# The expert layers of a two-block transformer kernel, as two phases with a scratch in DRAM between them

## The chip, the cores and the metric

The kernel runs on one NeuronCore of a Trainium2 chip (one of eight; the others are idle). The metric is the device time of one execution in microseconds (us). Engines are named as the profile names them: PE (TensorE) multiplies matrices, PEld is its weight load, DVE is VectorE, ACT is ScalarE, POOL is GpSimd, SP is SyncE, which here only issues DMAs. A kernel's launch is one program with one instruction stream for each engine; the streams are ordered by semaphores alone, written out by hand.

## The reference, cut to what matters

Two blocks follow one another. The first has two layers (DEPTH = 2), and each of them ends in a product-key mixture of experts over T = 256 tokens of width D = 1024. A query finds, for each token and each of 8 heads, 16 of 128 x 128 experts and their softmax weights:

```python
def one_block(xblk):
    q = (xblk @ w_query).reshape(B, TOKEN_BLOCK, N_PEER_HEADS, 2, SUBKEY_DIM)
    s = jnp.einsum('bthpd,hpnd->bthpn', q, sub_keys).astype(jnp.float32)
    vals, idx = lax.top_k(s, PEER_TOPK)
    ...
    top_s, pos = lax.top_k(cand, PEER_TOPK)
    eidx = jnp.take_along_axis(cand_idx, pos, axis=-1)
    g = jax.nn.softmax(top_s, axis=-1).astype(xblk.dtype)
    h = jnp.einsum('btd,bthkd->bthk', xblk, expert_u[eidx])
    act = jax.nn.gelu(h, approximate=False) * g
    return jnp.einsum('bthk,bthkd->btd', act, expert_v[eidx])
```

The kernel gathers nothing. It multiplies all tokens with all 16384 rows of `expert_u` (128 tiles of 128 experts), takes the gelu, multiplies with a dense gate (tokens x experts, zero where an expert wasn't chosen) and multiplies the result with all rows of `expert_v`. Beside that there are modulation vectors: `silu(c) @ ada_w` for both blocks, matrices of 1024 x 6144 and 1024 x 9216 per layer.

## The kernel before, in words

**Weights.** Every weight comes as units of 128 partitions x 1024 floats (512 KB) through one ring of four buffers (`raw`), loaded by SP in a fixed order: unit q goes to buffer q % 4, and its load waits until unit q - 4 has been used. A matrix product in full precision is made of three products of a reduced type: ACT copies a unit's halves to the high part (`hi`, L529, tile `wh`), DVE subtracts for the low part (`lo`, L954, tile `wl`), and PE multiplies three times (L1620 to L1622 for a tile of `expert_u`, `w_in` and the like; L1675 to L1677 for rows of `expert_v`). `wh` and `wl` have four half slots, so they hold two units. A raw buffer of such a unit is free when both `lo` halves are done. The units of the modulation matrices ("ada") are used by PE as they are: four plain float32 products side by side in four column strips (L1773, helper `ada`), or with 12 columns of vectors at a time (L1793, helper `rows_times`).

**One expert layer before.** It has three stages one after another.
- Choices: DVE finds the top 16 of 16 lists and then of the candidates, for both halves of the tokens (L1263 to L1329). PE meanwhile runs 48 ada units (`ada1.1` in layer 0, `ada2_choice.1` in layer 1), then turns the choices (L1940).
- Gates: 64 batches of 4 tokens. DVE writes two one-hot matrices and a weighted one (L1357, L1359, L1361), ACT the low part of the weighted one (L791), PE multiplies them in eight products (L1955, L1956), and ACT copies the bank to the gates in the arena (L798). 48 more ada units run between the batches (L1793, `ada2_gates`).
- Pairs (helper `pairs` with nin = 1, 128 pairs): PE multiplies a tile of `expert_u` while ACT takes the gelu of the one before (L583), DVE multiplies it with the gate (L1365) and splits it in high and low (L1012, L1014), and PE multiplies the result with the rows of `expert_v` into four accumulating banks. The units come as u0, u1, v0, u2, v1 and so on.

**Memory.** The gates fill the arena (128 KB of each partition), which also holds the scores and lists of the choices until the gates overwrite them. The one-hots of the gates stand in `wh`, `wl`, `AG` and `AP_`, so no weights can be split while gates are made.

**Around it.** Before a layer come the mixing products and `query`, then the scores (L1926, L773). After layer 0 the accumulated sum goes back to X and layer 1 begins; after layer 1 POOL loads tables and the second block's feed-forward stages begin, with `pairs` and nin = 2, which the change leaves as it is.

Of the kernel before, what the change touches and what calls it, by code (L numbers as in the profile page):

```python
# [56 lines left out]
ADA2_GATES = 6  # L57
ADA2_CHOICE = (0, 6)
ADA2_FIRST = (0, ADA2_CHOICE[0] + ADA2_GATES)

# [9 lines left out]
def plan():  # L70
# [17 lines left out]

    add("ada1.0", 48, False)
    for l in range(DEPTH):  # L90
# [7 lines left out]
        if l == 0:  # L98
            add("ada1.1", 48, False)
        if ADA2_CHOICE[l]:  # L100
            add(f"ada2_choice.{l}", KT * ADA2_CHOICE[l], False)
        add(f"ada2_gates.{l}", KT * ADA2_GATES, False)
        add(f"experts.{l}", 2 * KEYS, True, KEYS)
# [11 lines left out]
    out, q, s, r, g = {}, 0, 0, 0, 0  # L115
    for name, units, split, source, groups in rows:
        out[name] = Stage(name, units, split, source, q, s, r, g)
        q += units
        s += units * split
        r += units * (not split)  # L120
        g += groups
    return out, placed
# [70 lines left out]
def build(nc, ctx, stream, columns, tables, x_in, ctx_in, rpb, out):  # L193
    stages, _ = plan()
# [17 lines left out]
    AH = sb("AH", [P, 2, T], F32R)  # L212
    AL = sb("AL", [P, 2, T], F32R)
    AG = sb("AG", [P, 2, T])
    AP_ = sb("AP_", [P, 2, T])
# [14 lines left out]
    cs2 = sb("cs2", [P, KT, 2])  # L230
# [7 lines left out]
    weight_hi = sb("weight_hi", [P, T], F32R)  # L238

    MOST_ROWS = 2 * max(ADA2_GATES, *ADA2_CHOICE)  # L240
    pick = sb("pick", [P, KT, 2 + MOST_ROWS])
    rows = sb("rows", [P, UNIT])
# [36 lines left out]

    def one_hots(k):  # L280
        k = k % 2
        return (wh[:, k, :], (AG, AP_)[k][:, :, :].rearrange("p a w -> p (a w)"), wh[:, 2 + k, :], wl[:, k, :])
# [39 lines left out]
    rows_copied = sem("rows_copied")  # L322
    picked = sem("picked")
    mod_turned = sem("mod_turned")
    mod_copied = sem("mod_copied")
# [46 lines left out]
    hot_step = sem("hot_step")  # L372
    low_ready = sem("low_ready")
# [11 lines left out]
    BATCH = 4  # L385
    BATCHES = T // BATCH
    ROUND = BATCHES // ADA2_GATES // 2 * 2
    REST = range(ROUND * ADA2_GATES, BATCHES)

# [3 lines left out]
    def mod_places(name):  # L393

        return 0 if name.startswith("ada1") else 64

    ADA_STAGES = sum(name.startswith("ada") for name in stages)

    def pair_steps(nin):
        count = KEYS if nin == 1 else FF_TILES  # L400
        body = 2 if nin == 1 else 4
        rounds = (count - 1) // body
        return count, body, rounds
# [3 lines left out]
    def _(sp):  # L407
        seen = Seen()

        def released(unit):  # L410

            for st in stages.values():
                if st.q <= unit < st.q + st.units:
                    k = unit - st.q
                    return (lo_ready, 2 * (st.s + k) + 2) if st.split else (raw_used, st.r + k + 1)


# [4 lines left out]

        for st in stages.values():

            for k in range(4 if st.units >= 4 else st.units):
# [28 lines left out]
    def _(pool):  # L454
# [9 lines left out]
        picks = [0]  # L464
        read_by = [0]

        def pick_vectors(name, nv):

            st = stages[name]
            vectors = cs[:, 0, :].unsqueeze(2) if nv == 1 else cs2[:, :, :]  # L470
            zeros = spread(head_pick[:, 0:nv], KT)
            if read_by[0]:
                pool.wait_ge(raw_used, read_by[0])
            pool.memset(pick[:, :, :], 0.0).then_inc(picked, 1)
            pool.wait_ge(picked, picks[0] + 1)
# [8 lines left out]
        for l in range(DEPTH):  # L484
# [4 lines left out]
            if l == 0:  # L489
                pool.wait_ge(silu_ready, 1)  # L490
# [25 lines left out]
    def _(act):  # L516
# [52 lines left out]
        def pairs(st, nin, func, hooks=None, then=None):  # L569
# [18 lines left out]
            if nin == 2:  # L588
                hi(st, 1)
# [346 lines left out]
    def _(dve):  # L936
# [55 lines left out]
        def pairs(st, nin, combine, hooks=None, then=None):  # L992
# [26 lines left out]
            if nin == 2:  # L1019
                lo(st, 1)  # L1020
# [1257 lines left out]
```

## Time and profile before

| | us |
|---|---|
| median of 3 runs | 4233.03 (4229.99 to 4234.79) |
| the profiled execution | 4228.66 |
| its span (first to last instruction on the core) | 4226.9 |
| PE busy | 3918.0 (93%) |
| DVE busy | 2746.0 (65%) |
| ACT busy | 1996.5 (47%) |
| mean rate of the DMAs | 169 GB/s |

Busy time of PE is from start to modelled end of pipelined products, so two that overlap count once. A weight load (PEld) runs beside the product before it. A plain float32 product has two records each for PE and PEld. "Idle before, releaser" tells what ended an engine's idle time. PEclk is the granted clock of PE as a share of full speed: 1.00 is 2.4 GHz throughout, 0.50 is 1.2 GHz throughout.

### The profile page before, as it was taken

What the parts mean: (1) busy time and instruction counts of PE and PEld (TensorE: products, weight loads), DVE (VectorE), ACT (ScalarE), POOL (GpSimd) and SP (SyncE); (2) the same over time, 40 slices, a digit from 0 to 9 for tenths busy, and PEclk for the clock granted to TensorE, in tenths of its full rate; (3) what the DMA queues carried; (4) which work ended last, traced back from release to release, by engine and by line L of the source; (5) the groups of instructions that cost most, each with busy time, mean ns of one, the idle gap of its engine ahead of it and who ended that gap; (6) DMA issues with size and microseconds to landing.
All of it is one profiled execution on the core that took longest, in us unless ns stands there. A gap on an engine that the chain in (4) does not pass through costs nothing.

```text
span 4226.9 us, 77624 instructions
## 1 busy us (share of the span) xinstructions
PE 3918.0 (93%) x25828; PEld 3362.6 (80%) x25828; DVE 2746.0 (65%) x5370; ACT 1996.5 (47%) x3973; POOL 96.7 (2%) x96
## 2 busy tenths in 40 slices
PE   6989499999999999859999999989999989898998
PEld 2989146999999888714799999979998779898897
DVE  1563976776667665597676677756666665666665
ACT  1554065445544554327554445444454444444444
POOL 0000000000000000000000000001001010101010
PEclk6999599999999999869999999999999999999999
DMA  8435644555555434654455555565554225454453
GB/s 285 153 112 170 243 145 146 186 188 185 188 187 186 163 115 150 209 184 164 153 186 186 188 185 187 186 193 184 167 186 137 93 66 186 140 186 139 140 179 134
DMA packets 195903, 714.34 MB, mean 169 GB/s; under 512 B 21696, under 2 KB 22080, under 8 KB 195520
## 3 DMA queue, kind: packets, MB, share of 16 engines
q1 hardware_dynamic: 194112, 705.08, 50.0%
q0 software_dynamic: 1664, 7.57, 0.7%
q8 instruction: 79, 1.29, 0.1%
q14 instruction: 48, 0.39, 0.0%
HBM read 711.52 MB, written 1.05 MB: 169 GB/s over the span
## 4 chain that ended last, share of the span: by engine, by line
PE 84%; DVE 10%; ACT 2%; DMA 2%; issue 1%; PEldq 0%; SPq 0%; DVEq 0%; ACTq 0%; PEld 0%; POOL 0%
PE bank L1620 16%; PE bank L1622 16%; PE bank L1621 16%; PE bank L1675 8%; PE bank L1676 8%; PE bank L1677 8%; PE bank L1793 4%; PE bank L1955 2%; PE bank L1738 2%; DMA raw<-stream 2%; PE bank L1956 1%; DVE wl L954 1%; PE bank L1926 1%; PE bank L2080 1%; DVE arena L1318 0%
## 5 line engine op out<-in xcount | busy, mean ns | idle before, releaser
L954 DVE TENSOR_TENSOR wl<-raw,wh 128x512 fp32r<-128x512 f32 x2180 | 1508.0, 704 | 1032.0 <-ACT wh L529 999.1
L529 ACT ACTIVATE wh<-raw 128x512 fp32r<-128x512 f32 x2180 | 1345.6, 630 | 1214.0 <-PE bank L1622 758.4
L1620 PE MATMUL bank<-XH,wh 128*128 128x256 f32 x5184 | 1499.3, 289 | 94.3 <-DVE XL L1056 46.1
L1621 PE MATMUL bank<-XL,wh 128*128 128x256 f32 x5184 | 1483.5, 286 | 0.0
L1622 PE MATMUL bank<-XH,wl 128*128 128x256 f32 x5184 | 1483.0, 286 | 0.0
L1620 PEld LDWEIGHTS bank<-XH,wh 128*128 128x128 f32 x5184 | 1008.9, 195 | 129.3 <-issue 79.1
L1621 PEld LDWEIGHTS bank<-XL,wh 128*128 128x128 f32 x5184 | 1012.0, 195 | 14.0 <-issue 1.0
L1622 PEld LDWEIGHTS bank<-XH,wl 128*128 128x128 f32 x5184 | 1010.9, 195 | 0.0
L1675 PE MATMUL bank<-wh,AH 128*128 128x512 f32 x1464 | 574.4, 392 | 0.0
L1676 PE MATMUL bank<-wl,AH 128*128 128x512 f32 x1464 | 573.9, 392 | 0.0
L1677 PE MATMUL bank<-wh,AL 128*128 128x512 f32 x1464 | 569.6, 389 | 0.0
L1677 PEld LDWEIGHTS bank<-wh,AL 128*128 128x128 f32 x1464 | 275.0, 188 | 60.1
L1675 PEld LDWEIGHTS bank<-wh,AH 128*128 128x128 f32 x1464 | 276.3, 189 | 49.0 <-issue 0.7
L1676 PEld LDWEIGHTS bank<-wl,AH 128*128 128x128 f32 x1464 | 276.3, 189 | 43.4
L565 ACT ACTIVATE arena<-bank 128x256 f32 (+1 forms) x208 | 79.9, 384 | 320.0 <-PE bank L1622 319.9
L1773 PE MATMUL bank<-raw,vectors 128*32 128x256 f32 x1152 | 145.0, 599 | 87.2 <-DMA raw<-stream 83.5
L1955 PEld LDWEIGHTS bank<-wh 128*128 128x128 f32 x512 | 102.6, 200 | 129.3 <-issue 90.0
L1793 PE MATMUL bank<-raw,pick 128*12 128x512 f32 x384 | 189.6, 607 | 0.0
L1773 PEld LDWEIGHTS bank<-raw,vectors 128*32 128x32 f32 x1152 | 29.0, 136 | 192.9 <-DMA raw<-stream 154.0
L1365 DVE TENSOR_TENSOR AP_<-AG,arena 128x256 f32<-128x256 f32 x256 | 160.0, 625 | 10.9 <-ACT AG L583 10.9
L1014 DVE TENSOR_TENSOR AL<-AP_,AH 128x256 fp32r<-128x256 f32 x366 | 156.0, 426 | 12.5
L1620 PE MATMUL bank<-X2H,wh 128*128 128x256 f32 x544 | 156.1, 287 | 2.9 <-DVE wl L954 2.9
(237 smaller groups left out, 3458.5 us busy)
## 6 DMA issues: line engine op xcount, KB each, us to landing
raw<-stream SPq DMA_DIRECT2D x1340, 512.0 KB, 3.3
arena<-rpb POOLq DMA_DIRECT2D x4, 1024.0 KB, 20.5
arena<-tables POOLq DMA_DIRECT2D x2, 832.0 KB, 7.4
X<-x_t SPq DMA_DIRECT2D x1, 1024.0 KB, 7.6
arena<-ctx_t POOLq DMA_DIRECT2D x1, 1024.0 KB, 6.4
out_t<-X SPq DMA_DIRECT2D x4, 256.0 KB, 2.1
arena<-tables POOLq DMA_DIRECT2D x1, 608.0 KB, 8.8
cols<-columns SPq DMA_DIRECT2D x1, 218.0 KB, 2.5
```

Of the source, the lines that this page charges most:

```text
L529: act.activation(wh[:, n % 4, :], raw[:, q % 4, HALF * half:HALF * (half + 1)], ACT.Copy).then_inc(hi_ready, 1)
L954: tt_op(wl[:, n % 4, :], raw[:, q % 4, HALF * half:HALF * (half + 1)], wh[:, n % 4, :].bitcast(F32), SUB).then_inc(lo_ready, 1)
L1365: return tt_op(AP_[:, j % 2, :].unsqueeze(2), AG[:, j % 2, :].unsqueeze(2), gates[:, :, bass.ds(j + body * i, 1)], MUL)
L1620: pe.matmul(out, wh[:, n % 4, a:b], moving_h, start=start, stop=False, skip_group_check=check)
L1621: pe.matmul(out, wh[:, n % 4, a:b], moving_l, start=False, stop=False, skip_group_check=check)
L1622: return pe.matmul(out, wl[:, n % 4, a:b], moving_h, start=False, stop=stop, skip_group_check=check)
L1675: pe.matmul(out, high, wh[:, n % 4, :], start=first, stop=False)
L1676: pe.matmul(out, high, wl[:, n % 4, :], start=False, stop=False)
L1677: last = pe.matmul(out, low, wh[:, n % 4, :], start=False, stop=final)
L1773: matmul = pe.matmul(banks[6 + b % 2][GROUP * g:GROUP * (g + 1), 0:BLOCK], vectors[:, kt, :], raw[:, q % 4, BLOCK * g:BLOCK * (g + 1)], st ...
L1793: matmul = pe.matmul(banks[6 + half][0:n_rows, :], pick[:, kt, nv:nv + n_rows], raw[:, q % 4, HALF * half:HALF * (half + 1)], start=first ...
L1955: pe.matmul(banks[k % 2][:, at], high[:, at], hot_j[:, at], start=True, stop=False)
```

## The change

Each expert layer is done in two phases.

Phase 1: all 128 tiles of `expert_u` are multiplied first. Each result gets its gelu (ACT, to `HS`) and is stored by a DMA from ACT's queue to `h_spill` in DRAM (128 KB per tile). Between the tiles PE runs 96 ada units (all of both stages before), four for each five tiles in the first 120; the ring's order mixes them in the same way. DVE's choices are cut into pieces of at most some 8 instructions with a `feed()` (the next tile's `lo`) between them. ACT's two exps stand at tiles 26 and 53, the turn of the choices on PE at tile 57, and one batch of gates is made with each tile from 60 on. The gates are now one plain float32 product for each token instead of two of the reduced type; ACT writes the weighted one-hot (four copies for a batch), DVE only the two plain ones. The one-hots have a space of their own (`side`), which AG, AP_, AH and AL share.

Phase 2: SP loads each result back from `h_spill` (four slots, `HV`) beside each unit of `expert_v`; DVE multiplies it with the gate, ACT makes its high part, DVE its low part, PE multiplies with the rows of `expert_v`.

The helpers `ada_rows`, `rows_times`, `turn` and the work of POOL for them go. Phase 1 is written out tile by tile, without loops; phase 2 has loops.

```diff
+    def mix(l, base):
+        u = out[f"expert_u.{l}"]
+        for k in range(MIXED_U):
+            ring[base + 9 * (k // 5) + 2 * (k % 5)] = (u, k)
+        for k in range(MIXED_U, KEYS):
+            ring[base + MIXED_A + k] = (u, k)
+        for a in range(MIXED_A):
+            st = out[MIXED_ADA[l][a // 48]]
+            ring[base + 9 * (a // 4) + 2 * (a % 4) + 1] = (st, a % 48)
...
-        add(f"experts.{l}", 2 * KEYS, True, KEYS)
+        for name in MIXED_ADA[l]:
+            add(name, 48, False)
+        add(f"expert_u.{l}", KEYS, True, KEYS)
+        add(f"expert_v.{l}", KEYS, True)
...
+        def load_values(l):
+            st = stages[f"expert_v.{l}"]
+            sp.wait_ge(onehots_free, 2 + BATCHES * (l + 1))
+            for j in range(8):
+                if j >= 4:
+                    sp.wait_ge(gate_done, KEYS * l + j - 3)
+                sp.wait_ge(h_stored[j % 2], 16 * (KEYS // 2 * l + j // 2 + 1))
+                load_h(l, j)
+                load(st.q + j)
...
+            for u in range(KEYS):
+                if u + 1 < KEYS:
+                    hi(U, u + 1)
+                else:
+                    hi(V, 0)
+                    row_highs(0)
+                if u:
+                    store_h(u - 1)
+                b = u - GATES_FROM
+                if 0 <= b < BATCHES:
+                    act.wait_ge(unweighted_ready, first + b + 1)
+                    act.wait_ge(onehots_free, first + b + 1)
+                    for n in range(BATCH):
+                        t = BATCH * b + n
+                        last = act.activation(by_weight[:, b % 2, n * P:(n + 1) * P], unweighted[:, n * P:(n + 1) * P],
+                                              ACT.Copy, scale=routed[:, 2, t:t + 1])
+                    last.then_inc(weighted_ready, 1)
+                group_done(U, u)
+                if l or u >= 2:
+                    act.wait_ge(h_stored[u % 2], 16 * (KEYS // 2 * l + u // 2))
+                act.activation(HS[:, u % 2, :], banks[4 + (U.g + u) % 2][:, 0:T], ACT.Gelu).then_inc(group_free, 1)
+                b = u - GATES_FROM - 2
+                if 0 <= b < BATCHES:
+                    act.wait_ge(onehots_free, 2 + first + b + 1)
+                    act.activation(A(b * HOT, HOT), banks[b % 2][:, :], ACT.Copy).then_inc(gate_banks_free, 1)
...
                 for n in range(LISTS):
                     step(nc.vector.match_replace(repl[:, n, :], vals[:, n, 0:8], scores[:, n, :], -3e38))
                     step(nc.vector.max_index(idxu[:, n, 0:8], vals[:, n, 0:8], scores[:, n, :]))
+                    if n % 3 == 2:
+                        feed()
...
+            for b in range(BATCHES):
+                feed()
+                if b or l:
+                    dve.wait_ge(weighted_ready, first + b)
+                tt_op(batch(unweighted), keys, over_tokens(0, b), ALU.is_equal).then_inc(unweighted_ready, 1)
+                dve.wait_ge(onehots_free, first + b + 1)
+                tt_op(batch(hot_j[:, b % 2, :]), keys, over_tokens(1, b), ALU.is_equal).then_inc(onehots_ready, 1)
...
+            with dve.Fori(0, KEYS // 4 - 1) as i:
+                for j in range(2, 6):
+                    lo(V, j, i, 4)
+                    row_lows(j, i)
+                    gated(j + 1, i, 4 * i)
...
+            for u in range(KEYS):
+                pe.wait_ge(group_free, U.g + u + 1)
+                tile(U, u, 0, 0, banks[4 + (U.g + u) % 2][:, 0:T], first_pair)
+                if u == 0:
+                    pe.wait_ge(route_evacuated, 8 * (l + 1))
+                for a in after(u):
+                    ada_unit(first_block + a // KT, a % KT, place[MIXED_ADA[l][a // 48], a % 48])
...
+                b = u - GATES_FROM - 1
+                if 0 <= b < BATCHES:
+                    spread_choices(b)
```

## Rows read from the trace of the kernel before

**Rows 1.** Busy times by stage: us, busy us (instructions), PEclk, DMA share, GB/s.

```profile
core 0: us, PE busy (x) PEld busy (x) DVE busy (x) ACT busy (x) POOL busy (x), PEclk, DMA share, GB/s
422.00:527.00 105.00, 51.05 (x399) 11.73 (x391) 103.72 (x416) 4.72 (x15) 0.00 (x0) 0.57 0.70 245
527.00:709.00 182.00, 167.65 (x725) 83.87 (x725) 124.17 (x201) 118.98 (x327) 1.68 (x10) 0.91 0.42 139
709.00:1428.00 719.00, 719.00 (x4599) 656.27 (x4600) 503.17 (x896) 358.83 (x640) 0.00 (x0) 1.00 0.56 186
1766.00:1871.00 105.00, 51.91 (x399) 11.90 (x399) 103.73 (x416) 4.76 (x15) 0.00 (x0) 0.56 0.69 245
1871.00:2054.00 183.00, 168.63 (x740) 85.46 (x739) 125.69 (x203) 120.62 (x328) 1.68 (x10) 0.92 0.42 140
2054.00:2771.00 717.00, 717.00 (x4591) 654.02 (x4591) 502.78 (x896) 357.19 (x638) 0.83 (x2) 1.00 0.57 186
```

**Rows 2.** PE in order of time: start us, us; first and last products of layer 0's experts.

```profile
420.84 0.28 PE L1926 MATMUL bank<-raw,arena 128*128 128x128 f32 x1
...
1429.89 0.39 PE L1677 MATMUL bank<-wh,AL 128*128 128x512 f32 x1
```

**Rows 3.** PE in order of time: the starts of one pair's halves and of the next pair.

```profile
1000.04 0.28 PE L1620 MATMUL bank<-XH,wh 128*128 128x256 f32 x1
...
1002.91 0.40 PE L1675 MATMUL bank<-wh,AH 128*128 128x512 f32 x1
...
1005.66 0.28 PE L1620 MATMUL bank<-XH,wh 128*128 128x256 f32 x1
```

**Rows 4.** Groups of instructions, 1000 to 1100 us: busy us, mean ns, idle before.

```profile
L954 DVE TENSOR_TENSOR wl<-raw,wh 128x512 fp32r<-128x512 f32 x72 | 49.7, 691 | 29.0 <-ACT wh L529 26.8
L529 ACT ACTIVATE wh<-raw 128x512 fp32r<-128x512 f32 x71 | 44.9, 632 | 50.2 <-PE bank L1622 29.0 <-PE bank L1677 21.3
L1365 DVE TENSOR_TENSOR AP_<-AG,arena 128x256 f32<-128x256 f32 x18 | 11.3, 626 | 0.0
L1014 DVE TENSOR_TENSOR AL<-AP_,AH 128x256 fp32r<-128x256 f32 x18 | 7.7, 425 | 0.6
L583 ACT ACTIVATE AG<-bank 128x256 f32<-128x256 f32 x18 | 6.6, 366 | 0.0
```

**Rows 5.** DVE in order of time: the first pieces of the choices and the last one.

```profile
421.78 3.19 DVE L1263 MAX8 arena<-arena 128x8 f32<-128x128 f32 x16 [19.19 <-ACT arena L773]
...
459.88 2.29 DVE L1315 TENSOR_TENSOR arena<-arena,iota 128x2048 f32<-128x2048 f32 x1
...
526.82 0.29 DVE L1329 TENSOR_TENSOR arena<-arena,small 128x128 f32<-128x128 f32 x1
```

**Rows 6.** PE in order of time: three ada units in a row (eight records each).

```profile
421.80 1.50 PE L1773 MATMUL bank<-raw,vectors 128*32 128x256 f32 x24 [0.69 <-ACT arena L773]
```

**Rows 7.** The chain that ended last: plain float32 products of 128 columns, two records each.

```profile
406.55 14.57 PE bank L1926 x128
```

**Rows 8.** PE and ACT in order of time, one batch of gates.

```profile
590.22 0.28 PE L1956 MATMUL bank<-wh,wl 128*128 128x128 f32 x1
...
590.43 1.89 PE L1793 MATMUL bank<-raw,pick 128*12 128x512 f32 x4
...
590.66 0.58 ACT L798 ACTIVATE arena<-bank 128x512 f32 x1
...
591.48 1.28 ACT L791 ACTIVATE wl<-AP_,routed 128x128 fp32r<-128x128 f32 x4 [0.24 <-DVE AP_ L1357]
```

**Rows 9.** DMAs of the ada stage at the start, 12 to 88 us, and its window.

```profile
12.00:88.00 76.00, 52.70 (x392) 11.12 (x388) 0.66 (x4) 3.66 (x14) 0.00 (x0) 0.66 0.95 334
...
raw<-stream SPq DMA_DIRECT2D x48, 512.0 KB, 5.0
```

**Rows 10.** DMAs among the pairs, 1000 to 1100 us: time to issue, time to landing.

```profile
L438 SPq DMA_DIRECT2D raw<-stream x35: 332/333/333, 1001.8 to 1097.3; - x35
...
DMA to landing us min/median/max: 3.0/3.2/3.5
```

**Rows 11.** Biases load in rows of 1 KB: window, then GB/s in 40 slices of 2771:2800.

```profile
2771.00:2796.00 25.00, 12.95 (x69) 11.47 (x67) 12.91 (x25) 9.94 (x18) 9.38 (x6) 0.73 1.02 263
...
GB/s 271 424 333 328 362 426 403 416 411 376 280 232 203 192 203 226 203 249 198 198 237 198 215 237 209 220 203 209 237 198 243 209 209 226 198 243 254 277 158 34
```

**Rows 12.** DMA issues of the page: the only stores, KB each, us to landing.

```profile
out_t<-X SPq DMA_DIRECT2D x4, 256.0 KB, 2.1
```

**Rows 13.** Waits, 709 to 1427 us: who waited for whom, us in total, times, longest.

```profile
DVE wl L954 <- ACT wh L529: 185.8, 250, 0.8
...
PE bank L1620 <- DVE wl L954: 1.7, 1, 1.7
```

**Rows 14.** Groups of the page: loads of ACT's function table at gelu and at exp.

```profile
L583 ACT ACT_TABLE_LOAD x8 | 10.3, 1283 | 0.1
L782 ACT ACT_TABLE_LOAD x2 | 2.6, 1283 | 0.2
```

More of the change, by code:

```diff
@@ L113, in plan @@
     add("ffn.1.1", 3 * FF_TILES, True, FF_TILES)
-    out, q, s, r, g = {}, 0, 0, 0, 0
+    out, ring, q, s, r, g = {}, {}, 0, 0, 0, 0
     for name, units, split, source, groups in rows:
         out[name] = Stage(name, units, split, source, q, s, r, g)
+        if name.startswith("expert_u"):
+            l = int(name[-1])
+            mix(l, out[MIXED_ADA[l][0]].q)
+        elif not any(name in names for names in MIXED_ADA):
+            for k in range(units):
+                ring[q + k] = (out[name], k)
         q += units
@@ L190, in __call__, with build @@
         return self.at[name]
-def build(nc, ctx, stream, columns, tables, x_in, ctx_in, rpb, out):
-    stages, _ = plan()
+def build(nc, ctx, stream, columns, tables, x_in, ctx_in, rpb, h_spill, out):
+    stages, ring, _ = plan()
+    place = {(st.name, k): q for q, (st, k) in ring.items()}
     made = operands_made()
@@ L384, in build, with after, block_after @@
     SLOTS = 4
-    BATCH = 4
     BATCHES = T // BATCH
-    ROUND = BATCHES // ADA2_GATES // 2 * 2
-    REST = range(ROUND * ADA2_GATES, BATCHES)
     block = ctx.enter_context(nc.Block())
[L393 to L403, printed above, removed]
+    BLOCKS_PER_LAYER = MIXED_A // KT
+    def after(u):
+        return [4 * (u // 5) + u % 5] if u < MIXED_U and u % 5 < 4 else []
+    def block_after(u, late):
+        n, rest = divmod(u - late - 8, 10)
+        return n if rest == 0 and 0 <= n < BLOCKS_PER_LAYER else None
     @block.sync
@@ L408, in _, with released, load @@
         seen = Seen()
[L410 to L415, printed above, removed]
+        def released(q):
+            st, k = ring[q]
+            return (lo_ready, 2 * (st.s + k) + 2) if st.split else (raw_used, st.r + k + 1)
+        def load(q):
+            st, k = ring[q]
+            if q >= 4:
+                sp.wait_ge(*released(q - 4))
+            sp.dma_start(raw[:, q % 4, :], stream[st.source + k, :, :]).then_inc(raw_ready[q % 4], 16)
         sp.dma_start(cols[:, :], columns).then_inc(prepared, 16)
@@ L1822, in _ @@
+        pe.wait_ge(silu_ready, 1)
+        for k in range(48):
+            ada_unit(k // KT, k % KT, stages["ada1.0"].q + k)
+            if k > KT and k % KT == 1:
+                turn_block(k // KT - 1)
+        turn_block(5)
+        pe.wait_ge(block_placed, 6)
         for l in range(DEPTH):
```

502 lines of the change are left out of this document (228 added, 274 removed).

## The prediction

> **What bounds the kernel now.** I read the busy times by stage first. The 719 us of pairs have PE busy for all of it at the full clock; the reader should see that nothing in them is to be had from a shorter wait [rows 1, 13]. The two stages ahead of them are different. In the 105 us of choices DVE is busy for 103.7 and PE for 51, at a clock of 0.57; in the 182 us of gates PE is busy for 168, but with eight small products for each batch and with ada products of 12 columns [rows 1]. So DVE bounds the first, PE the second, and the ada units are long work on PE in one and cheap, DMA-fed work in the other. The last product of the scores starts at 420.8 and the last one of the experts ends at about 1430: 1009 us for layer 0, which the change rebuilds [rows 2]. Layer 1 has the same stages within 2 us [rows 1]; I take 1007. All else (some 2210 us) I cost at nothing: its code is the same.
>
> **Prices.** A tile of u takes 2.87 us of PE, a row of v 2.75 (1002.91 - 1000.04 and 1005.66 - 1002.91) [rows 3]. An ada unit in column strips takes 1.50 / 3 = 0.50 [rows 6]. A change between reduced and plain type costs 0.1 on each side (the ada product starts 0.21 after the last gate product where 0.11 would be the pace) [rows 8]. So a unit between two tiles is 0.6 or so, taking a side's cost twice and some of the unit's tail as hidden. On DVE a `lo` half takes 0.69, the pair some 1.3 as they overlap; on ACT a `hi` half 0.63, the gelu 0.37 [rows 4].
>
> **Phase 1, tiles 0 to 59, with the choices.** Three resources come out alike.
> PE: five tiles and four units are 5 x 2.87 + 4 x 0.6 = 16.75 us, twelve times 201.
> DVE: the choices last from 421.8 to 526.8, 105 us [rows 5], and sixty `lo` pairs of 1.3 are 78: 183.
> DMA: nine units and five stores. At 334 GB/s, the rate when the ring does nothing else [rows 9], a unit of 0.524 MB is 1.57 us, nine are 14.1. A store of 0.131 MB in rows of 1 KB was never seen. The bounds are that rate (0.39) and some 210 GB/s, which is what the biases' rows of 1 KB get from a full set of engines in the later slices (0.6) [rows 11]; five stores are 2.0 to 3.1, the sum 16.1 to 17.2.
> None of them alone costs much over PE's 201, but they meet in a ring of four buffers in strict order. I walked through it. The first tile of a group of nine goes to the buffer that the third ada unit of the group before gives back; from there PE has two tiles and one unit left, 6.3 us. In these must fit the issue 0.33 and landing 3.2 with a quiet ring [rows 10], 5.0 with a full one [rows 9], then `hi` 0.63, the rest of a piece of choices on DVE (pieces last 1.4 to 2.4 us: eight of the 0.2 us that 3.19 / 16 gives, or one of 2.29 [rows 5]; half of that, 1.0, on average) and `lo` 0.7. That is 5.9 to 7.7. Where it is over 6.3, PE waits, and the third tile's load, which waits for this one's `lo`, is late again. Walked with a landing of 4.2 the group takes 17.9, with 5.0 19.5, and with 3.2 PE's 16.75. I take 18.3: 12 x 18.3 = 220. Six turns of a block (two transposes and their changes of type, 0.6) and the turn of the choices (1.8, with the copies) bring 5: **225**.
> ACT has little to do here: 1.3 + 0.37 + one store's issue, 0.33 if it is as on SP [rows 10], is 2.0 of 3.7. The two exps bring four loads of the table at 1.28 [rows 14], each pair beside a slack of 1.7; up to 1 us each, inside the rounding.
> A page speaks to the DMA line. The Trainium skill, "DMA: Bandwidth & Descriptors", section Specifications, puts the limit of HBM for one core at about 358 GB/s; by it a group's 5.4 MB would take 15.0 us instead of the row's 16.1, and the ring would be the easier side. The row decides.
>
> **Phase 1, tiles 60 to 127, with the gates.** A batch on PE is four plain products of 128 columns: 64 took 14.57, so 0.91 [rows 7], and 0.2 for changes of type: 1.1. It replaces eight of 0.11, so the gates' own products cost what they did. With 2.87 for the tile and 0.8 x 0.6 for ada a tile comes to 4.46. 64 of them, six block turns and the tile before the first batch: 285 + 3.6 + 2.9 = **292**. Three last tiles: **9**.
> Beside it, for each tile: DVE 1.3 + 2 x 0.69 = 2.7. ACT 1.3 (`hi`) + 0.33 (store) + 1.28 (four weighted copies) + 0.58 (bank to arena) [rows 8] + 0.37 (gelu) + 0.06 = 3.9. ACT works in order and waits for PE's tile ahead of the gelu, so it starts again 0.4 after it, and has 4.0 left for its 3.5: PE stays the bound by 0.5. If an issue on ACT costs nothing that is 0.9, if it costs 0.33 more and each handoff 0.2, ACT needs 4.7 and the region 16 us more; that is in the range. The ring has 8.3 us for the chain above, so it is at ease; 9 units and 5 stores per 22 us are 244 GB/s.
>
> **Phase 2.** 128 rows at 2.75: **352**. What must fit beside a row: DVE `lo` 1.3 + gate 0.63 + low part 0.43 [rows 4] = 2.4 (87%); ACT `hi` 1.3 + a high part of 128x256, priced by the gelu's 0.37: 1.7; DMA 0.655 MB, 239 GB/s, under 334 [rows 9] and under the 263 of the window of mixed rows [rows 11]. PE's row j waits for its low part. From PE's first half of row j - 2 the second half's `hi` can start after 1.37; `hi`, `lo`, low part end at 1.37 + 0.63 + 0.1 + 0.69 + 0.43 = 3.2, where PE wants it at 4.1; DVE's gate for j + 1 ends at 3.9 and the next `lo` is wanted at 3.5, so it slips by 0.4 and is caught up. Bounds: 2.75, and 4.1 if every step were serial (0.63 + 0.37 + 0.43 and two `hi`, `lo` halves at 0.63 and 0.69). I take the first: before, DVE waits only for ACT and PE never for either [rows 13]. The loads from `h_spill` have three rows of time, 8 us, the stores behind them long landed. A store has only the output's 256 KB in 2.1 us to go by [rows 12]; `HS` has two slots, so gelu u waits for store u - 2, issued 5 us before: it fits, even with the 5.0 of a full ring barely.
> On that same place the Trainium skill, "DMA: Bandwidth & Descriptors", section Anatomy of one DMA, speaks against the scratch: a fixed part of about 2.0 us in each DMA, most of it the receipt of the write, heaviest where the target is HBM. As an estimate by that page 128 KB would land in 2.3 us; the output's stores agree with it, and as it lies beside 6 us of tiles it would not change the sum.
> The handover costs 2 us (first high and low parts after the last gelu).
>
> **The sum.** 225 + 292 + 9 + 352 + 2 = 880 us for a layer, against 1009 and 1007: 129 + 127 = 256 less. The profiled execution of 4228.7 would become 3972; it lies 4.4 below the median of the runs, so I forecast 3972 + 4 and round to **3975**. What pays is the choices (105 us hidden) and the gates' idle and ada time; what is paid is ada units at 0.6 in PE's line and a ring that is nearly full.
>
> **Rivals.**
> A. PE bounds everywhere: the ring keeps up. Tiles 0 to 59 are then 206: 861 a layer, 3975 - 38 = 3937. For it: a landing of 3.2 where two transfers at most are in flight [rows 10]. Against: 318 of 334 GB/s are asked for [rows 9].
> B. The ring, in strict order, is worse than walked, and ACT's issue and handoffs bound the gates: 20.5 for a group (246) and 4.8 for a tile with gates (+22): 25 + 22 = 47 a layer, 4070. For it: DVE at 87% to 90% with pieces that can't be cut, ACT within 0.5.
> C. The slower end: phase 2 becomes a chain. The result goes from DVE to ACT and back to DVE, in order behind `lo` and `hi`. If nothing of it overlaps, a row takes 4.1 instead of 2.75: 173 more a layer, 1053, so 3975 + 346 = 4321, and from 3.75 us a row on the gain is gone (256 us over 256 rows, 1.0 more each). Against: the order on DVE puts the gate of j + 1 a full row ahead.
> D. The clock. In the stages of choices PE sat at 0.57 with half its time idle [rows 1]. If tiles 0 to 59 had gaps enough to fall to 0.9, their 201 us of PE work would be some 20 longer, 40 for both: 4015. I put it inside B and the range.
>
> **How the numbers follow.** Forecast (3940 to 4010) 0.50, A (under 3940) 0.17, B and D (4010 to 4150) 0.25, something between B and no gain 0.02, C 0.06. The range leaves out C and the far ends of A and B: 3915 to 4090. A measurement of this kernel can tell some 0.2%, 8 us. Faster 0.93, same 0.01, slower 0.06.
>
> **What would show it.** Phase 1 should begin at 421 and phase 2 at about 947; starts of u0, u60 and u124 at 421, 646, 938. Right: PE waits in tiles 0 to 59 for `lo`, and it for `hi` or for a DMA, at 290 to 300 GB/s; hardly any wait in phase 2, with rows 2.75 apart, DVE near 87%. Wrong: a gap ahead of every row of phase 2 that ends with DVE's low part (C); a landing of over 5 us and DMA share near 1 (B); PE waiting for ACT's weighted copies or bank copies in the gates (B); a PEclk under 1.00 in phase 1 (D). If the rest of the kernel moved by more than 5 us I would have missed something in it.

## The result and the profile after

The changed kernel takes 3936.37 us (median of 4, 3933.09 to 3938.61), the kernel before 4231.51 in the same session: a ratio of 0.9301, 95% interval 0.9285 to 0.9317, or 295 us less. The forecast was 3975 with a range of 3915 to 4090. The result lies in the range, but under the forecast's own bin (3940 to 4010, chance 0.50) and in that of rival A (under 3940, 0.17; priced at 3937). The profiled execution took 3933.09 us, and its span is 3931.2.

From the page of the profile after: busy times, clock, the chain that ended last, and how long the DMAs took to land (KB each, us). PE is at 95%, and PEclk no longer dips in the choices.

```profile
PE 3737.8 (95%) x26204; PEld 3329.4 (85%) x26204; DVE 2533.7 (64%) x4978; ACT 2048.9 (52%) x4251; POOL 92.6 (2%) x72
...
PEclk6999999999999999999999999899999999999999
...
PE 76%; PEld 6%; DVE 6%; DMA 5%; issue 3%; ACT 2%; PEldq 1%; SPq 0%; ACTq 0%; DVEq 0%; POOL 0%
...
raw<-stream SPq DMA_DIRECT2D x1340, 512.0 KB, 4.1
h_spill<-side ACTq DMA_DIRECT2D x256, 128.0 KB, 4.0
side<-h_spill SPq DMA_DIRECT2D x256, 128.0 KB, 3.8
```

The windows of layer 0, which answer to [rows 1] (columns as there): tiles beside the choices, tiles beside the gates, the last three tiles, phase 2.

```profile
422.00:643.00 221.00, 213.68 (x1856) 186.19 (x1856) 180.06 (x540) 100.32 (x200) 0.00 (x0) 1.00 0.87 294
643.00:924.00 281.00, 281.00 (x2467) 254.85 (x2466) 163.87 (x256) 202.32 (x528) 0.00 (x0) 1.00 0.71 241
924.00:932.00 8.00, 8.00 (x69) 8.00 (x68) 4.54 (x8) 4.54 (x10) 0.00 (x0) 1.00 0.91 311
932.00:1287.00 355.00, 351.43 (x1557) 290.42 (x1557) 279.57 (x518) 203.09 (x389) 0.54 (x1) 1.00 0.76 241
```

DVE's 180 us of choices and `lo` now lie beside 214 us of PE work, where DVE's 103.7 us of choices had lain beside 51.05 of PE at a clock of 0.57 [rows 1]. The borders, from PE in order of time (start us, us; the idle time in brackets): tile 0, tile 60, tile 125, the first two rows of `expert_v`, two rows in the middle, the last product.

```profile
422.51 0.36 PE L1709 MATMUL bank<-XH,wh 128*128 128x256 f32 x1
...
642.03 0.28 PE L1709 MATMUL bank<-XH,wh 128*128 128x256 f32 x1
...
923.60 0.36 PE L1709 MATMUL bank<-XH,wh 128*128 128x256 f32 x1
...
932.46 0.47 PE L1764 MATMUL bank<-wh,AH 128*128 128x512 f32 x1
...
936.47 0.49 PE L1764 MATMUL bank<-wh,AH 128*128 128x512 f32 x1 [1.05 <-DVE AL L1441]
...
1100.48 0.39 PE L1764 MATMUL bank<-wh,AH 128*128 128x512 f32 x1
...
1103.20 0.39 PE L1764 MATMUL bank<-wh,AH 128*128 128x512 f32 x1
...
1281.81 0.39 PE L1766 MATMUL bank<-wh,AL 128*128 128x512 f32 x1
```

| layer 0, us | forecast | measured |
|---|---|---|
| tiles 0 to 59 | 225 | 219.5 (642.03 - 422.51) |
| tiles 60 to 124 | 292 | 281.6 (923.60 - 642.03) |
| last three tiles | 9 | 8.9 |
| phase 2 and handover | 354 | 349.7 (to 1281.81, and 0.39) |
| the layer | 880 | 859.7 |

Layer 1 repeats the first two terms as 219.8 and 281.6. The last product of layer 1's experts on PE, first in the kernel before, then in the one after:

```profile
2771.69 0.39 PE L1677 MATMUL bank<-wh,AL 128*128 128x512 f32 x1
```

```profile
2475.76 0.39 PE L1766 MATMUL bank<-wh,AL 128*128 128x512 f32 x1
```

At the end of layer 0 the changed kernel is 148.1 us ahead (1429.89 in [rows 2] less 1281.81), at the end of layer 1 295.9, and at the end of the span 295.7: nothing outside the two layers moved by as much as 1 us.

Who waited in tiles 1 to 59 (us in total, times, longest), and from 940 to 1280 us in phase 2:

```profile
ACT wh L561 <- DMA raw<-stream: 79.4, 53, 3.8
DVE wl L991 <- ACT wh L561: 37.8, 32, 3.9
...
PE bank L1709 <- ACT side L822: 4.0, 6, 1.5
```

```profile
ACT wh L561 <- PE bank L1766: 144.1, 251, 0.7
DVE wl L991 <- ACT wh L561: 69.4, 126, 0.6
```

ACT's `hi` waits for a load 53 times, up to 3.8 us: the ring is nearly full, as forecast. But the wait seldom gets through to PE. In 423 to 640 us PE stood idle for 7.3 us, all of it ahead of the group of L1709, which holds the first product of each tile (busy us, mean ns | idle before):

```profile
L1709 PE MATMUL bank<-XH,wh 128*128 128x256 f32 x474 | 139.1, 293 | 7.3 <-ACT side L822 4.0 <-DVE wl L991 3.3
```

Behind the handover (1.05 at 936.47) PE waits for nobody in phase 2: the list from 940 to 1280 us is the two lines above, and both are of engines that are ahead of PE, as in the pairs before [rows 13].

### The profile page after: what moved, and what is told of

The parts are those of the page before. It is cut to its first block, busy times and chain, and to the rows that moved or that the text cites. A ratio compares the mean times of both kernels' runs of the same rounds, so it can differ in the third digit from the quotient of the medians.

```text
span 3931.2 us, 75611 instructions
## 1 busy us (share of the span) xinstructions
PE 3737.8 (95%) x26204; PEld 3329.4 (85%) x26204; DVE 2533.7 (64%) x4978; ACT 2048.9 (52%) x4251; POOL 92.6 (2%) x72
## 4 chain that ended last, share of the span: by engine, by line
PE 76%; PEld 6%; DVE 6%; DMA 5%; issue 3%; ACT 2%; PEldq 1%; SPq 0%; ACTq 0%; DVEq 0%; POOL 0%
PE bank L1709 16%; PE bank L1710 16%; PE bank L1711 16%; PE bank L1764 5%; PE bank L1765 5%; PE bank L1766 5%; DMA raw<-stream 4%; PE bank L1981 3%; PE bank L1849 3%; PEld bank L1764 2%; PEld bank L1766 2%; DVE wl L991 2%; PEld bank L1765 2%; PE bank L1827 2%; ACT wh L561 1%
## 5 line engine op out<-in xcount | busy, mean ns | idle before, releaser
L991 DVE TENSOR_TENSOR wl<-raw,wh 128x512 fp32r<-128x512 f32 x2180 | 1483.3, 702 | 883.9 <-ACT wh L561 880.0
L561 ACT ACTIVATE wh<-raw 128x512 fp32r<-128x512 f32 x2180 | 1317.4, 628 | 978.0 <-PE bank L1766 437.0
L1709 PE MATMUL bank<-XH,wh 128*128 128x256 f32 x5184 | 1519.1, 293 | 107.2 <-DVE XL L1092 48.4
L1709 PEld LDWEIGHTS bank<-XH,wh 128*128 128x128 f32 x5184 | 1006.3, 194 | 169.0 <-issue 87.8
L1426 DVE TENSOR_TENSOR side<-iota,routed 128x512 f32<-128x512 f32 x128 | 88.6, 692 | 199.5 <-PE bank L1981 199.5
L822 ACT ACTIVATE side<-bank 128x256 f32<-128x256 f32 x256 | 97.9, 382 | 218.0 <-PE bank L1711 207.2
L1849 PE MATMUL bank<-raw,vectors 128*32 128x256 f32 x1920 | 172.0, 434 | 35.9 <-DMA raw<-stream 35.3
L816 ACT ACTIVATE side<-side,routed 128x128 f32<-128x128 f32 x512 | 162.8, 395 | 0.0
L1433 DVE TENSOR_TENSOR side<-side,arena 128x256 f32<-128x256 f32 x256 | 159.3, 622 | 0.0
L1709 PE MATMUL bank<-X2H,wh 128*128 128x256 f32 x544 | 156.0, 287 | 2.9 <-DVE wl L991 2.9
L1710 PE MATMUL bank<-X2L,wh 128*128 128x256 f32 x544 | 154.7, 284 | 0.0
```

Source lines behind the costliest of these rows:

```text
L561: act.activation(wh[:, n % 4, :], raw[:, q % 4, HALF * half:HALF * (half + 1)], ACT.Copy).then_inc(hi_ready, 1)
L816: last = act.activation(by_weight[:, b % 2, n * P:(n + 1) * P], unweighted[:, n * P:(n + 1) * P], ACT.Copy, scale=routed[:, 2, t:t + 1])
L991: tt_op(wl[:, n % 4, :], raw[:, q % 4, HALF * half:HALF * (half + 1)], wh[:, n % 4, :].bitcast(F32), SUB).then_inc(lo_ready, 1)
L1433: tt_op(AP_[:, j % 2, :].unsqueeze(2), HV[:, j % 4, :].unsqueeze(2), gates[:, :, bass.ds(j + more, 1)], MUL).then_inc(gate_done, 1)
L1709: pe.matmul(out, wh[:, n % 4, a:b], moving_h, start=start, stop=False, skip_group_check=check)
L1710: pe.matmul(out, wh[:, n % 4, a:b], moving_l, start=False, stop=False, skip_group_check=check)
```

## The experiments

Each kernel differs from the changed one (3936.4 us) by the edit shown. Differences that matter are read inside a phase, since a phase 1 of the same code took 510.0 and 510.3 us (layers 0 and 1) in the changed kernel, and 509.9 and 517.1, 515.3 and 515.2, 510.6 and 513.2 in three kernels that differ from it only in phase 2. So 5 to 10 us of a total can be this alone.

### Are the choices hidden, and at what price?

The choices run in one piece, with no `lo` between their instructions.

```diff
+            pause = [True]
             def feed():
+                if pause[0]:
+                    return
...
+            pause[0] = False
             while fed[0] <= EXP_AT[TT - 1]:
                 feed()
```

> The pieces of the choices on DVE run in one block; the splitting of the next tiles (feed) begins only behind them. Nothing is left out. Theory P (PE's line is full; what the change gained is that the choices lie beside tiles, and their pieces cost PE almost nothing): each layer gets back nearly the whole 105 us of choices, less the at most two tiles that PE has at hand (6) and the 7 us that PE waits now in tiles 0 to 59, plus some 3 us for the clock after the gap: +95 a layer, 4126 in all, with 150 us PE-idle in place of 7 ahead of tile 2. Rival G (most of the gain is the shorter gates and the cheaper ada units, and the pieces now stretch tiles 0 to 59 as much as they are hidden, by 18 us a layer): +75 a layer, 4086 or less.

4148.09 us, ratio 0.9796 (0.9778 to 0.9814): 212 us more, 106 a layer, which is 22 us over the first theory's 4126 and far over rival G's 4086. PE's busy time in the window 423 to 528 of this kernel is 3.35 us, and the clock falls to 0.52:

```profile
423.00:528.00 105.00, 3.35 (x23) 2.76 (x22) 103.19 (x406) 2.05 (x4) 0.00 (x0) 0.52 0.04 14
```

The whole of the choices comes back into the path, so cutting them in pieces hides about all of their 105 us. This one part is 212 of the 295 us gained. The other 83, which come from the gates and the ada units, no run takes apart.

The same run shows what the pieces cost the tiles, and it isn't what was expected. From tile 2 to tile 52 (532 to 720 us) the choices are over but for a few short pieces, and PE waits no less:

```profile
532.00:720.00 188.00, 180.37 (x1548) 158.11 (x1547) 64.75 (x101) 80.19 (x163) 0.00 (x0) 0.98 0.85 289
...
L1714 PE MATMUL bank<-XH,wh 128*128 128x256 f32 x406 | 120.1, 296 | 7.6 <-ACT side L822 5.7 <-DVE wl L991 2.0
```

It is 7.6 us of idle time in 188, at 289 GB/s and with DVE busy for a third of it, against 7.3 in 217 with the choices beside the tiles. So most of the waits in tiles 0 to 59 come with the ring's loads and not with the pieces of the choices. The expectation had counted on these 7 us to go, which is a good part of its miss of 11 a layer.

### What an ada unit costs, and whether the ring takes it back

The 48 ada units beside the choices, and the 48 beside the gates, stand in twos after tiles 1 and 3 of five, instead of alone after tiles 0, 1, 2 and 3.

```diff
+def ada_at(u):
+    return 2 * (u < MIXED_U and u % 5 in (1, 3))
```

> Ada units in twos, after tiles 1 and 3 of each five, in the ring too, instead of one after each of tiles 0 to 3. Theory P (PE's line is full, and a change between reduced and plain products costs it some 0.2 to 0.3 us): the second unit of a pair costs 0.43 instead of 0.76 in tiles 0 to 59 and 0.43 instead of 0.57 beside a gate batch: 24 x 0.33 + 23 x 0.14 = 11 us a layer less, 3914. Theory R (as predicted: in tiles 0 to 59 the ring of four buffers sets the pace at 18.3 us for nine units): the group keeps its 18.3 or grows, as two ada units must have landed together; gain at most the 3 us of the gates' part: 3930 to 3950.

3926.68 us, ratio 0.9269 (0.9257 to 0.9282): 10 us less, between the two numbers. The same window and the same group of PE as above, in this kernel:

```profile
423.00:640.00 217.00, 200.62 (x1796) 180.58 (x1795) 172.90 (x525) 93.45 (x192) 0.00 (x0) 1.00 0.85 291
```

```profile
L1720 PE MATMUL bank<-XH,wh 128*128 128x256 f32 x465 | 134.4, 289 | 16.3 <-ACT side L833 12.7 <-DVE wl L1002 3.4
```

PE has 9 us less to do (200.6 against 209.7 in the same 217 us) and stands idle for 9 more: tiles 0 to 59 took 223.0 against 219.5, and 226.7 against 219.8 in layer 1. The gain is all in the tiles beside the gates, where the ring has time: 273.6 against 281.6. So both theories held, each in its own stage.

In fours after tile 3 of five:

```diff
+def ada_at(u):
+    return 4 * (u < MIXED_U and u % 5 == 3)
```

> Ada units in fours, after tile 3 of each five. Theory P alone, if the ring had no say: 36 x 0.33 + 35 x 0.14 = 17 us a layer less, 3902. Theory R: the fifth tile's load waits for the first of the four ada units to be used, and from there needs 4.4 to land, 0.6 for the high and 0.7 for the low part, while PE has 1.3 us of ada left: a wait of 4.4 us for each of 24 groups, 105 a layer, 3902 + 210 = 4112.

4087.08 us, ratio 0.9652 (0.963 to 0.9674): 151 us more, 25 under the ring theory's 4112. PE waits for the gelu's bank to come free, which is behind a `hi` that waits for its load for up to 7.5 us (us in total, times, longest; 423 to 640 us):

```profile
ACT wh L572 <- DMA raw<-stream: 66.3, 11, 7.5
...
PE bank L1720 <- ACT side L833: 32.8, 9, 4.1
```

The ring's chain is real, and the spacing of the ada units is what keeps it off PE. Part of the 151 us is the clock: with these gaps it is 0.90 in 423 to 640 us, where it was 1.00.

### What the scratch costs

The stores to `h_spill` and the waits on them are left out; the loads of phase 2 stay, with the same bytes, but read other data. The kernel leaves out that the expert results reach phase 2.

```diff
-                act.wait_ge(group_free, 2 + U.g + u + 1)
-                act.dma_start(h_spill[u, :, :], HS[:, u % 2, :]).then_inc(h_stored[u % 2], 16)
+                return
...
-            sp.dma_start(HV[:, j % 4, :], h_spill[j, :, :]).then_inc(h_loaded[j % 4], 16)
+            sp.dma_start(HV[:, j % 4, :], stream[stages[f"expert_u.{l}"].source + j, :, 0:T]).then_inc(h_loaded[j % 4], 16)
```

> The stores to the scratch are left out, with the waits on them; the loads of phase 2 read as many bytes from another place (the first 1 KB of each row of expert_u's units), so the result isn't the product of the gelus. Theory P: PE gets back only the 4 us a layer in which it waits for a gelu that waited for its slot to be stored: 3928 (3924 to 3932). Theory R: 10% of the DMA share goes in tiles 0 to 59, a unit lands in 4.2 instead of 4.9, and a group of nine gets shorter by 0.7 to 1.2 us: 12 a layer, 3912. A third view, that the stores disturb more than their bytes (rows of 1 KB beside 4 KB ones), gives over 20 a layer, under 3896.

3918.36 us, ratio 0.9251 (0.9237 to 0.9265): 18 us less, 9 a layer, between the two. Phase 1 took 504.9 and 507.4 us instead of 510.0 and 510.3, phase 2 348.5 twice instead of 349.7 and 349.8. In 423 to 640 us the DMAs move 266 GB/s instead of 296, a unit lands in 4.3 us instead of 4.9, and PE's idle time is 3.4 instead of 7.3:

```profile
L1703 PE MATMUL bank<-XH,wh 128*128 128x256 f32 x486 | 142.3, 293 | 3.4 <-ACT side L816 2.6 <-DVE wl L985 0.8
```

So the stores have a price, but the traces place only 10.5 of the 18 us, 5.1 of them in phase 1 of layer 0, where PE's idle time is 3.9 shorter. The rest is within what a phase 1 of the same code varies by. The ring theory's 12 us a layer isn't reached.

Whether it matters which of the two stands first on ACT, the store or the `hi`:

```diff
+                if u:
+                    store_h(u - 1)
                 if u + 1 < KEYS:
                     hi(U, u + 1)
...
-                if u:
-                    store_h(u - 1)
```

> Only ACT's order changes: the store of tile u - 1 is issued ahead of hi(u + 1), not behind it, so that it no longer waits for that tile's load. If the 4 us a layer in which PE waits for a gelu come from the store's late issue (gelu u waits for the slot of store u - 2), they go: 3928. If the load of the next tile is what both wait for, nothing changes: 3936. If ACT's stall at the head of the queue for the gelu's end plus 0.33 for the issue holds up the splits, PE waits more for them: 3940 to 3950.

3938.99 us, ratio 0.9303 (0.9288 to 0.9318): no change that can be measured, and the 3936 and the 3940 of the expectation can't be told apart. The gelu waits for a store and the `hi` for a load, and their order moves neither.

### Where the ada units should stand

24 ada units of a layer beside the choices, in twos after tile 2 of five, and 72 beside the gates, in twos after tiles 0, 2 and 4.

```diff
+def ada_at(u):
+    return 2 * (u % 5 == 2) if u < 60 else 2 * (u < MIXED_U and u % 5 in (0, 2, 4))
```

> Ada units in twos again, but only 24 of a layer's 96 in tiles 0 to 59 (two after tile 2 of each five) and 72 beside the gates (two after tiles 0, 2 and 4 of each five). The runs so far: a lone ada unit costs PE 0.76 wherever it stands, one of two 0.59; in tiles 0 to 59 with twos PE saved 9 us and gave it back in waits, beside the gates it kept 8. Theory PR (PE's line is full, and the ring of four takes back what is saved only where it is asked for 9 units in 18 us): here both parts have air in the ring (7 units in 15.5 us, 11 in 22.4), so the whole 96 x 0.17 = 16 us and half of the 7 us of waits are kept: 19 a layer, 3898. Rival V (DVE takes over in tiles 0 to 59: 105 us of choices and 78 of splits in 191 of PE): the part can't go under some 200, gain 8 less: 3914. Rival S (it isn't the ring but gelus held up by stores): no more than e2, 3927.

3908.94 us, ratio 0.9233 (0.922 to 0.9246), the fastest kernel here, 27 us under the changed one and between the first theory's 3898 and rival V's 3914. Of the 27, 10 are what the twos alone gave, so moving 24 units gave 18. Its two windows of layer 0:

```profile
424.00:624.00 200.00, 196.18 (x1699) 184.95 (x1698) 181.83 (x546) 100.06 (x204) 0.00 (x0) 1.00 0.78 269
624.00:919.00 295.00, 291.41 (x2674) 265.46 (x2674) 167.45 (x259) 200.00 (x533) 0.00 (x0) 1.00 0.78 276
```

Both parts now ask for some 270 GB/s, where the changed kernel asked for 296 and 241 and the one in twos for 291 and 250 (644 to 918 us), and PE is idle for under 4 us in each. Tiles 0 to 59 take 194.4 us and tiles 60 to 124 293.6.

All 96 beside the gates:

```diff
+def ada_at(u):
+    return 2 * (60 <= u < MIXED_U and u % 5 != 3)
```

> No ada unit in tiles 0 to 59, all 96 of a layer beside the gates, in twos after the tiles 0, 1, 2 and 4 of five. Against the version with 24 of them in tiles 0 to 59 (3908.9 us, 201.5 us from the first tile to the first spread product of a layer, 295.3 from there to the first row of phase 2). PE theory: PE's work is the same wherever the units stand, so only its idle 3.8 us a layer can go: 181 us for the first part, 309.5 for the second, 3901 to 3905. DVE theory: with nothing else on PE's line the 105 us of choices and the lo halves (1.3 us a tile) hold the tiles at 186 to 190, 5 to 9 us of PE stand still in each layer, and the time is 3911 to 3920, no better than with 24 units there.

3959.4 us, ratio 0.9348 (0.9334 to 0.9362): 50 us worse than the version before, far more than either theory gave. The windows of layer 0, then the waits from 619 to 946 us:

```profile
425.00:618.00 193.00, 185.39 (x1517) 180.59 (x1515) 179.71 (x544) 95.65 (x195) 0.00 (x0) 1.00 0.68 214
618.00:946.00 328.00, 311.34 (x2870) 272.27 (x2863) 168.25 (x260) 203.50 (x541) 0.00 (x0) 1.00 0.83 286
```

```profile
ACT wh L572 <- DMA raw<-stream: 118.2, 47, 6.0
...
PE bank L1720 <- DVE wl L1002: 13.3, 21, 1.5
```

The first part, from tile 0 to the first product of the gates, took 194.3 us, where PE's work alone was put at 181 and DVE's hold at 186 to 190. PE waits in it behind pieces of the choices (its idle time is 7.6 us, 6.4 of it ended by `lo`), so the DVE theory had the direction and was short by 4 us. The miss is in the second part, 327.5 us instead of 309.5: it asks for 286 GB/s, and there the ring's waits return, in a stage where DVE is busy for half the time. They go with the rate and the spacing, not with the choices.

Threes after tiles 1 and 3 beside the gates, and the first part as in the version of 3908.9 us:

```diff
+def ada_at(u):
+    return 2 * (u % 5 == 2) if u < 60 else 3 * (u < 120 and u % 5 in (1, 3))
```

> As the version of 3908.9 us in tiles 0 to 59 (24 ada units in twos), but the 72 beside the gates stand in threes after tiles 1 and 3 of five instead of twos after 0, 2 and 4. From units alone (0.76) and in twos (0.59) one change of product type and back costs 0.34 and a unit 0.42, so in threes a unit should take 0.53. PE theory: 72 x 0.06 = 4 us a layer less, 3901. Ring theory: three units leave the ring in 1.6 us and take 4.7 us to load at 334 GB/s, so the tiles behind them wait for their data as they did with fours: no gain or a loss, 3909 to 3940.

3919.57 us, ratio 0.926 (0.9248 to 0.9273): 11 us worse, so no gain, as the ring theory said. From tile 62 to tile 120 of layer 0 the threes took 266.7 us and the twos 266.7 (894.27 - 627.53 and 892.01 - 625.36); PE has less to do but idles for 6.7 us from 627 to 922, where with twos it idles for 3.6 from 624 to 919. In layer 1 the threes took 272.6 for the same tiles and the twos 265.9, which is the larger part of the 11 us. Another 3.3 lie in tiles 0 to 59 of layer 0, whose code is the same (197.7 against 194.4 us); what makes that differ is open.

### What phase 2 can bear

Rival C said that phase 2 could become a chain. To find DVE's slack, one to three extra subtractions, whose results nobody reads, are put behind the low part of each row from row 2 on.

```diff
+                if j >= 2:
+                    for n in range(1):
+                        tt_op(rows[:, n * T:(n + 1) * T], AP_[:, j % 2, :], AP_[:, j % 2, :], SUB)
```

> Phase 2: one subtraction of 128x256 more on DVE for each row, behind the low part, into unused memory. It measures how far the rows are from the chain of rival C. DVE is busy for 2.18 us of a row's 2.72 and would be at 2.56. Theory P (rows are PE's; handoffs have the slack of the walk, 0.9 us at the low part and 0.5 in DVE's time): no change, 3936 to 3940. Rival C in part (DVE and ACT hand over with no slack): 0.38 for each of 252 rows, 4032.

3943.37 us, ratio 0.9309 (0.9295 to 0.9323). From the first row of layer 0 to the first tile of layer 1 it is 683.8 us here (1615.52 - 931.68) and 683.7 in the changed kernel (1616.12 - 932.46), so the operation costs nothing. Phase 2 took 349.5 and 350.1 us instead of 349.7 and 349.8. The 7 us of the total are no more than noise, as the two ratios' intervals overlap, and in the profiled execution 6.8 of them lie in layer 1's phase 1, 517.1 against 510.3 us, which is the same code.

> As e7, but two subtractions a row: DVE needs 2.94 us a row, more than PE's 2.72. Theory P: DVE sets the pace from here, 0.22 to 0.3 a row, +55 to +75: 3990 to 4012. Rival C in part: 0.76 a row, 4128.

3948.98 us, ratio 0.9325 (0.9307 to 0.9342): 12.6 us more, where 54 to 76 were expected. Phase 2 took 353.8 and 353.9 us, 8 more for both layers or 0.03 a row, and each phase 1 took 5 us more by itself. The expectation added the whole length of each record. In order of time on DVE (start us, us) the records overlap:

```profile
1101.80 1.27 DVE L991 TENSOR_TENSOR wl<-raw,wh 128x512 fp32r<-128x512 f32 x2
1103.01 0.41 DVE L1441 TENSOR_TENSOR AL<-side,AH 128x256 fp32r<-128x256 f32 x1
1103.34 0.74 DVE L1444 TENSOR_TENSOR rows<-side 128x256 f32<-128x256 f32 x2
1104.01 0.62 DVE L1433 TENSOR_TENSOR side<-side,arena 128x256 f32<-128x256 f32 x1
1104.56 1.27 DVE L991 TENSOR_TENSOR wl<-raw,wh 128x512 fp32r<-128x512 f32 x2
```

From start to start an extra subtraction takes 0.335 (two in 0.67, 1103.34 to 1104.01), though its record says 0.41. Without them DVE's row is 2.76 - 0.67 = 2.09 us of the 2.72, and not the 2.4 of the prediction. Two more fill it, and DVE is busy for all of 340 us:

```profile
940.00:1280.00 340.00, 338.54 (x1479) 270.57 (x1478) 339.99 (x741) 207.07 (x372) 0.00 (x0) 1.00 0.73 238
```

A third, of 128x128, decides between a slack that goes on and a bound that is reached:

```diff
+                    for n in range(2):
                         tt_op(rows[:, n * T:(n + 1) * T], AP_[:, j % 2, :], AP_[:, j % 2, :], SUB)
+                    tt_op(spare[:, :], AP_[:, j % 2, 0:128], AP_[:, j % 2, 0:128], SUB)
```

> Phase 2 with two extra DVE subtractions of 128x256 and a third of 128x128 in each row from row 2 on. With two of them DVE was busy for all of 340 us in the middle of phase 2 and a row took 2.75 us. Theory that a row costs what its busiest engine has to do: DVE is now the bound and each further operation adds its own time, 0.17 to 0.25 us a row, 43 to 63 us for 252 rows: 3992 to 4012. Theory that only a serial chain can hold phase 2 (the forecast's rival, from 3.75 us a row on) or that DVE has slack still: 3949 to 3956.

3989.54 us, ratio 0.9427 (0.941 to 0.9445), 40.6 more than with two. Phase 2 took 377.2 and 378.4 us instead of 353.8 and 353.9, 48 more or 0.19 a row (2.95 instead of 2.76), which is inside the 43 to 63 expected of the DVE bound. The whole kernel shows only 41, since its two phases 1 were 7 us shorter (510.6 and 513.2 against 515.3 and 515.2). An operation begins to cost its full time where DVE's row passes PE's:

```profile
960.00:1280.00 320.00, 320.00 (x1305) 236.46 (x1306) 320.00 (x762) 179.94 (x327) 0.00 (x0) 1.00 0.69 223
```

So phase 2 is bound by the busier of PE (2.72) and DVE (2.09), not by a chain. PE shows 320 of 320 busy here though DVE sets the pace. Of the four first products of a row, one has a record of 0.49 us instead of 0.39, so the mean is 416 ns instead of 390. PE's busy share alone would have hidden the wait. PEld's share fell from 83% to 74% (264.97 of 320 us in the changed kernel, 236.46 here).

## Why the prediction was right where it was, and what it had wrong

**The mechanism held.** The choices are hidden (212 us of the kernel by the first experiment), the clock stays at 1.00, nothing else in the kernel moved, and phase 2 runs at PE's pace. The time is inside the range. It is 39 us under the forecast, 20 a layer, and by its size it is rival A. A's reason, a ring that keeps up everywhere, is not quite what happened: A had tiles 0 to 59 at 206 us, and they took 219.5. That the total meets A's 3937 is luck.

**Tiles 0 to 59: 225 forecast, 219.5 measured, from three terms that were all off.** An ada unit between tiles was put at 0.6. The tiles of the changed kernel start 3.61 to 3.64 apart with a unit and 2.88 without one (tile 126), so it costs 0.76. PE's floor is 12 x (4 x 3.63 + 2.88) = 209 and not 201. The first step that was mis-sized is the price of the change of type: I had taken 0.1 for each side from one place [rows 8] and counted part of the unit's tail as hidden. PE in order of time, first an ada unit between two tiles, then a batch of gates between two tiles:

```profile
443.98 0.28 PE L1711 MATMUL bank<-XH,wl 128*128 128x256 f32 x1
444.19 0.64 PE L1849 MATMUL bank<-raw,vectors 128*32 128x256 f32 x8
444.76 0.38 PE L1709 MATMUL bank<-XH,wh 128*128 128x256 f32 x1
444.98 0.28 PE L1710 MATMUL bank<-XL,wh 128*128 128x256 f32 x1
```

```profile
903.61 0.28 PE L1711 MATMUL bank<-XH,wl 128*128 128x256 f32 x1
903.73 1.06 PE L1981 MATMUL bank<-side 128*128 128x128 f32 x8
904.55 0.36 PE L1709 MATMUL bank<-XH,wh 128*128 128x256 f32 x1
```

The products of a tile start 0.12 apart. The ada unit starts 0.21 after the last of them, 0.1 late as I had it, but the tile behind it is late as well: its first product comes 0.57 after the unit's start instead of 0.50, and the second 0.22 after the first. The batch, which is plain float32 too, starts 0.12 after the tile and so pays nothing on entry. What costs may then be the unit's column strips and not the type; no run tests that alone. Against the higher floor, the walk through the ring gave 19 us of waits, and PE waited 7.3. The landing in this stage is 4.9 us, almost the 5.0 that would have made a group 19.5 by the walk, yet a group took 18.3, so the walk was too severe at a given landing, and its 18.3 is met only because two errors cancel. I took a piece of choices to stand in the way of each `lo` by 1.0, but with hardly any choices beside the tiles PE waits as much (7.6 us in the first experiment). The turns, put at 5, are 1.6: a tile with a block turn takes 0.20 more, five times, and the turn of the choices 0.6. The last 2 us of the 219.5 are waits that the idle time doesn't show, as a product's record covers the first 0.16 us of each.

**Tiles 60 to 124: 292 forecast, 281.6 measured.** A tile with a batch and no ada unit takes 3.77 (904.55 - 900.78, tile 119), so a batch is 0.89 and not 1.1: 64 x 0.21 = 13 less. That is the 0.91 of its eight records [rows 7] with no change of type at all. The ada unit is 4.53 - 3.77 = 0.76, as beside the choices, so 48 of them are 36.5, 6 more than put down. A block turn is 0.18 to 0.22 and not 0.6, 2 us less for all. The sum of these is 9 to 10 less. PE waited for nobody, so the bound by PE was right, and ACT was busy 202 of 281 us, 3.1 a tile.

**Phase 2: 354 forecast, 349.7 measured.** The rows are 2.72 apart, not 2.75: 128 x 0.03 = 4. That it is because no tile of `expert_u` stands between them any more is likely, not shown. The handover was 1.05 instead of 2. That DVE had more room than thought (2.09 a row) changes nothing in the sum but moves rival C further away: its point of decision, 3.75 us a row, would need five extra operations of 0.335.

**The sum.** 5.5 + 10.4 + 0.1 + 4.3 = 20 a layer, 41 for both: 3975 - 41 = 3934, and 3936 was measured. The largest mis-sized term is the gates' batch (13 us a layer), ahead of the ring's waits (19 against some 9), on which the forecast and rivals A and B turned. One figure against rival A was a little off: a group of nine units and five stores in 16.75 us is 321 GB/s and not 318, and 296 were moved.

**The scratch.** The stores land in 4.2 us (median) beside the choices and in 3.5 beside the gates. The Trainium skill, "DMA: Bandwidth & Descriptors", section Anatomy of one DMA, from which 2.3 was estimated, isn't borne out at either place. Its figures are for DMAs issued from GpSimd, and these are issued from ACT beside the ring's loads. The output's stores, which the prediction says agree with it, don't quite: as an estimate by that page 256 KB would take 2.6 us, and they took 2.1 [rows 12]. Which part of the 18 us that go with the stores is their bytes, their landing or their issue on ACT, no run shows. On the limit of HBM (the same page, section Specifications) the trace says little: the stage moves 296 GB/s in the mean and has slices of up to 343, under the 358 of the page, but the slices of [rows 11] reach 426.

**Left open.** Why the same phase 1 takes 510 to 517 us in different kernels, and how the waits grow between 270 and 290 GB/s. No run changed the number of the ring's buffers or the length of the pieces of the choices, and none took the gates' share of the gain apart.

## What to carry to other kernels

Serial work of an engine that feeds others can hide nearly in full if it is cut into short pieces with the feeding between them. Then read what each stage asks of the ring and put loads that can wait where the rate is lowest: moving 24 units from a stage at 291 GB/s to one at 250 gave 18 us, and moving 24 more lost 50. Price an operation by the distance from start to start in its new place, not by its record or its pace in a row: for DVE 0.335 instead of 0.41, for an ada unit 0.76 instead of 0.50. And test the slack of a phase by adding work to it until the pace changes.

## What the runs showed of the hardware

- Placing four plain float32 column-strip products between reduced products costs 0.76 us of PE's line, alone or ahead of a batch. In twos ahead of a batch it is 0.60 for each (tiles of 4.96 us against 3.77), in threes 0.54 (5.39 against 3.77), against 0.50 in a row [rows 6].
- A batch of four plain float32 products of 128 columns, eight records, costs 0.89 us between a reduced tile and the next, no more than the 0.91 of its records in a row [rows 7].
- A ring of four buffers of 512 KB leaves PE idle for 3.4 to 3.8 us in 200 to 217 at 266 to 269 GB/s, 7.3 at 296, 16.3 at 291 when the plain units stand in twos, and 16.7 (in 328) at 286 when the ada units come in twos after four of five tiles. With units alone it is 7.6 in 188 at 289 though DVE is two thirds idle. So the spacing counts beside the rate.
- Records of DVE overlap by some 0.07 us (0.41 long, 0.335 apart), and where DVE set the pace PE's records still covered 320 of 320 us, so busy time can read as full on both.
